# Expert blocks of 32 rows in four column tiles, with the output projection one block behind

## The reference

```python
group = argmax(h2 @ w_rg)                     # one of 4 groups for a token
top2 of softmax((h2 @ w_re)[group])           # two of its 8 experts
gates = group_gate * top_p / sum(top_p)
# every token goes to its 2 experts: 4096 slots over 32 experts
out = (silu(xb @ w_g[e]) * (xb @ w_u[e])) @ w_d[e]     # 1024 -> 512 -> 1024
x = x + sum over the two slots of gates * out
```

## Time and profile before

| | us |
|---|---|
| median of 3 runs (3032.55 to 3043.99) | 3043.69 |
| profiled execution: own time | 3044.74 |
| profiled execution: span | 3043.0 |
| TensorE busy in the span | 2849.8 (94%) |
| VectorE busy | 1205.5 (40%) |
| ScalarE busy | 997.1 (33%) |
| GpSimd busy | 657.3 (22%) |
| first expert product | 2081.0 |
| last copy of y begins | 3035.9 |

### The profile page before, as it was taken

The page is one execution under the profiler, slowest core; times in us unless marked ns, Lnnn a source line. Parts: engine busy times, 40 slices in busy tenths (PEclk is TensorE's granted clock), DMA queues, the critical chain, the costliest instruction groups (busy, mean ns, idle before and its releaser), DMA issues. The chain is left out here.

```text
span 3043.0 us, 74182 instructions
## 1 busy us (share of the span) xinstructions
PE 2849.8 (94%) x29606; PEld 1672.9 (55%) x29607; DVE 1205.5 (40%) x2075; ACT 997.1 (33%) x1998; POOL 657.3 (22%) x857
## 2 busy tenths in 40 slices
PE   8999999999999997888888889968999999999998
PEld 3444444444666664777777645544555555555554
DVE  2333311113887875677666424351111111111111
ACT  1111100002666665555545333431222222222221
POOL 0000300000110112656555200002222222222222
PEclk9999999999999998999999999978999999999999
DMA  3211131111122030111111055414868778677763
GB/s 129 69 52 58 50 114 62 62 56 72 34 67 67 8 97 16 30 47 41 40 42 43 12 189 203 156 62 154 319 224 293 244 266 285 211 237 237 265 236 76
DMA packets 172755, 374.77 MB, mean 123 GB/s; under 512 B 28386, under 2 KB 109794, under 8 KB 153475
## 3 DMA queue, kind: packets, MB, share of 16 engines
q10 hardware_dynamic: 31088, 182.46, 15.3%
q1 hardware_dynamic: 128338, 146.25, 14.8%
q0 software_dynamic: 13120, 43.00, 6.8%
HBM read 298.79 MB, written 72.88 MB: 122 GB/s over the span
## 5 line engine op out<-in xcount | busy, mean ns | idle before, releaser
L2214 PE MATMUL gu_ps<-wg_,xT 128*64 128x128 f32 (+1 forms) x1760 | 391.1, 381 | 1.8 <-issue 1.8
L2215 PE MATMUL gu_ps<-wu_,xT 128*64 128x128 f32 (+1 forms) x1760 | 391.1, 381 | 0.0
L712 DVE TENSOR_TENSOR_SCAN h_all<-h_all 128x512 f32<-128x512 f32 (+3 forms) x320 | 345.9, 1129 | 68.9 <-ACT h_all L664 42.8
L344 PE MATMUL ps<-low,high 128*128 128x512 f32 x768 | 337.3, 596 | 2.4 <-issue 2.4
L2214 PEld LDWEIGHTS gu_ps<-wg_,xT 128*64 128x64 f32 x1760 | 220.2, 137 | 191.6 <-issue 191.5
L2235 PE MATMUL y_ps<-wd_,hT 128*64 128x512 f32 x648 | 295.4, 598 | 0.0
L2234 PE MATMUL y_ps<-wd_,hT 128*64 128x512 f32 x648 | 295.4, 598 | 0.0
L2309 DVE SCALAR_TENSOR_TENSOR h<-sil,gate,gu_ps 64x384 f32<-64x384 f32 (+1 forms) x162 | 78.9, 487 | 431.3 <-ACT sil L2266 431.3
L344 PEld LDWEIGHTS ps<-low,high 128*128 128x128 f32 x768 | 144.4, 191 | 173.2 <-issue 173.2
L1707 PE MATMUL ps<-high 128*128 128x512 f32 x512 | 232.3, 604 | 7.8 <-DMA high<-mixT 7.6
L2215 PEld LDWEIGHTS gu_ps<-wu_,xT 128*64 128x64 f32 x1760 | 220.2, 137 | 0.0
(11 more groups left out here) (315 smaller groups left out, 5018.2 us busy)
## 6 DMA issues: line engine op xcount, KB each, us to landing
wd_<-in_w_exp_down ACTq DMA_DIRECT2D x29, 2048.0 KB, 18.7
wg_<-in_w_exp_gate ACTq DMA_DIRECT2D x20, 2048.0 KB, 8.8
wu_<-in_w_exp_up ACTq DMA_DIRECT2D x20, 2048.0 KB, 14.1
high<-in_w_exp_gate ACTq DMA_DIRECT2D x9, 2048.0 KB, 8.9
high<-in_w_exp_up ACTq DMA_DIRECT2D x9, 2048.0 KB, 14.1
pT<-low SPq DMA_DIRECT2D x13, 1024.0 KB, 3.9
rkv<-pT SPq DMA_DIRECT2D x96, 128.0 KB, 2.4
high<-in_x SPq DMA_DIRECT2D x16, 512.0 KB, 4.0
```

Of the source, the lines that this page charges most:

```text
L344: done = pe.matmul(qkv_ps[:, part, :], hT[:, s, k, :], w_sb[:, k, part * SBW:(part + 1) * SBW], start=(k == 0), stop=(k == KT - 1))
L712: dve.tensor_tensor_scan(prod[:, n % KEPT, h, 0:w][:, ::-1], rows, rows, so_far, ALU.mult, ALU.bypass).then_inc(scanned, 1)
L2214: pe.matmul(gu_ps[half][LO, 0:wide], xT[:, k, :], wg[s][:, k, cols], start=(k == 0), stop=(k == KT - 1))
L2215: last = pe.matmul(gu_ps[half][HI, 0:wide], xT[:, k, :], wu[s][:, k, cols], start=(k == 0), stop=(k == KT - 1))
```

## The change

- Blocks of 32 rows. Each expert has at least two blocks, and the last one's number is made so that the total is even (`n_pairs`). Tables have 196 columns for 130.
- Four column tiles of 32 columns of the array: gate's two halves of 256 columns and up's two halves side by side into the four partition quarters of one PSUM bank `gu_ps`; the output projection likewise in four quarters of 256 columns.
- The output projection of block b-1 stands behind gate and up of block b; the transposes of h of block b-1 stand in the middle of gate and up of block b.
- Rows are fetched as quarters (four partitions per row, 256 values each) and added as quarters. For that `h2` is stored with each half of a row permuted (`by_chunk`), the router's weights are read in the same order, and the tables are spread to 128 partitions by one more product. Two buffers each of `take`, `put`, `gate` and `y`; one of `xg`, `xT`, `h`, `hT`.
- An add is issued when all adds before it are done, which GpSimd itself now waits for; it no longer waits for its fetch.
- SyncE issues the weight loads, when the down product of an expert's last block is done.

The diff, cut: what is removed from `run_experts` stands in the code above.

```diff
@@ -36,10 +36,10 @@
 N_GROUPS, PER_GROUP = 4, 8
 NE = N_GROUPS * PER_GROUP
 FF = 512
-ROWS = 64
-MAX_BLOCKS = 2 * SEQ // ROWS + NE
+ROWS = 32
+MAX_BLOCKS = 2 * SEQ // ROWS + 2 * NE
 SLOTS = 3
-TABLE = MAX_BLOCKS + SEQ // ROWS + 2
+TABLE = MAX_BLOCKS + 4
 NORM_EPS, LN_X_EPS = 1e-6, 64e-5
 EXP_HALF = 0.6065306597126334
@@ -1708,6 +1708,12 @@
                              start=(k == 0), stop=(k == KT - 1))
         if half == 1 and k == KT - 1:
             done.then_inc(self.mixed, 1)
+def by_chunk(row):
+    return row.rearrange("t (p k) -> t k p", p=P)
@@ -1905,7 +1913,11 @@
                     dve.wait_ge(rooted, t + 1)
                     dve.reciprocal(rstd[:, :], root[:, :])
                     dve.drain()
-                    dve.scalar_tensor_tensor(h2[:, s, :], x_t[:, s, :], rstd[:, :], gain[:, :], ALU.mult, ALU.mult).then_inc(h2_ready, 1)
+                    for half in range(2):
+                        cols = slice(512 * half, 512 * half + 512)
+                        done = dve.scalar_tensor_tensor(h2[:, s, cols].rearrange("t (k p) -> t k p", p=P), by_chunk(x_t[:, s, cols]), rstd[:, :],
+                                                        by_chunk(gain[:, cols]), ALU.mult, ALU.mult)
+                    done.then_inc(h2_ready, 1)
                 def one_tile(t, s, n, first, last):
...
@@ place_slots @@
-                dve.tensor_scalar(blocks[:, :], blocks[:, :], 1.0, None, ALU.max)
+                dve.tensor_scalar(blocks[:, :], blocks[:, :], 2.0, None, ALU.max)
...
+                pe.wait_ge(to_ready, 1)
+                pe.matmul(to_ps[:, 0:TABLE], spread[:, :, :].rearrange("t q r -> t (q r)"), to_f[:, :], start=True, stop=True).then_inc(spread_done, 1)
...
@@ -2096,60 +2133,72 @@
     with ExitStack() as ctx:
         sb, pb, sem = makers(nc, ctx, program)
         FT = FF // P
...
+        QUARTERS = [slice(q * ROWS, (q + 1) * ROWS) for q in range(4)]
+        LO, HI = slice(0, 2 * ROWS), slice(2 * ROWS, 4 * ROWS)
         wg, wu, wd = experts.wg, experts.wu, experts.wd
         gu_loaded, d_loaded = experts.gu_loaded, experts.d_loaded
...
+        take = [sb(f"take7{j}", [P, 1], I32) for j in range(2)]
+        put = [sb(f"put7{j}", [P, 1], I32) for j in range(2)]
+        gate = [sb(f"gate7{j}", [P, 1]) for j in range(2)]
+        xg = sb("xg", [P, 2, P])
+        xT = sb("xT", [P, 2, 4, ROWS])
+        sil = sb("sil", [P, FF // 2])
+        h = sb("h7", [P, FF // 2])
+        hT = sb("hT7", [P, 2, 2, ROWS])
+        y = [sb(f"y7{j}", [P, D // 4]) for j in range(2)]
         ident = sb("ident7", [P, P])
         warm = sb("warm7", [P, 1])
...
+        xT_ps = [pb(f"xT_ps7{j}", [P, 512]) for j in range(2)]
+        gu_ps = pb("gu_ps7", [P, 512])
+        hT_ps = pb("hT_ps7", [P, 512])
         y_ps = pb("y_ps7", [P, 512])
         names = """consts gathered turned xT_ready gu_done silu_ready h_ready h_turned hT_ready
...
+        def pairs_of_blocks(eng, pairs, one_block):
+            for b in range(4):
+                one_block(b, b % 2, first=(b == 0))
+            with eng.Fori(2, pairs) as i:
+                for j in range(2):
+                    one_block(i * 2 + j, j, first=False)
+        def stores_done(eng, blocks):
+            if not isinstance(blocks, int) or blocks > 0:
+                eng.wait_ge(stored, blocks * 16)
+        give_credit(nc, y_copied)
         with nc.Block() as block:
             @block.sync
             def _(sp):
+                def refill(e, s):
+                    sp.wait_ge(y_done, start_of(sp, e + 1))
+                    experts.load(sp, e + SLOTS, s)
                 experts.load(sp, SLOTS - 1, SLOTS - 1)
...
+                with sp.Fori(0, (NE - SLOTS) // SLOTS) as i:
+                    for s in range(SLOTS):
+                        refill(i * SLOTS + s, s)
+                for e in range((NE - SLOTS) // SLOTS * SLOTS, NE - SLOTS):
+                    refill(e, e % SLOTS)
             @block.gpsimd
             def _(pool):
@@ -2158,40 +2207,42 @@
                 pool.drain()
                 pool.sem_inc(consts, 1)
...
+                def gather(j):
+                    pool.indirect_dma_start(out=xg[:, :, :].rearrange("t a b -> t (a b)"), out_offset=None, in_=h2_quarters[:, :],
+                                            in_offset=bass.IndirectOffsetOnAxis(ap=take[j][:, 0:1], axis=0)).then_inc(gathered, 16)
+                def next_rows(j, b):
+                    pool.tensor_copy(take[j][:, :], from_all[:, bass.ds(b, 1)])
+                def one_block(b, j, first):
+                    pool.wait_ge(turned, b + 3)
+                    pool.sem_inc(on_pool, 1)
+                    gather(1 - j)
+                    next_rows(j, b + 4)
+                    pool.tensor_copy(put[j][:, :], to_all[:, bass.ds(b, 1)])
                     pool.drain()
...
+                    stores_done(pool, b)
+                    pool.sem_inc(on_pool, 1)
+                    pool.wait_ge(y_copied, b * 2 + CREDIT + 2)
+                    pool.sem_inc(on_pool, 1)
+                    pool.indirect_dma_start(out=out_quarters[:, :], out_offset=bass.IndirectOffsetOnAxis(ap=put[j][:, 0:1], axis=0),
+                                            in_=y[j][:, :], in_offset=None, compute_op=ALU.add).then_inc(stored, 16)
+                pairs = pairs_of(pool)
+                next_rows(0, 0)
+                next_rows(1, 1)
                 pool.drain()
...
+                gather(0)
+                for b in (1, 2):
+                    pool.wait_ge(turned, b)
+                    gather(b % 2)
+                    next_rows(1 - b % 2, b + 1)
+                    pool.drain()
+                pairs_of_blocks(pool, pairs, one_block)
+                pool.wait_ge(gathered, pairs * 32 + 48)
+                pool.sem_inc(on_pool, 1)
+                pool.wait_ge(stored, pairs * 32)
+                pool.sem_inc(on_pool, 1)
                 pool.drain()
@@ -2199,119 +2250,129 @@
                 def turn(b):
                     pe.wait_ge(gathered, b * 16 + 16)
                     pe.sem_inc(on_pe, 1)
...
+                    for j in range(2):
+                        last = pe.transpose(xT_ps[j][:, 0:P], xg[:, j, :], ident[:, :])
                     last.then_inc(turned, 1)
...
+                def gate_up(b, s, ks):
+                    for k in ks:
+                        for q, (w, half) in enumerate(((wg, 0), (wg, 1), (wu, 0), (wu, 1))):
+                            last = pe.matmul(gu_ps[QUARTERS[q], 0:256], xT[:, k % 2, k // 2, :], w[s][:, k, half * 256:(half + 1) * 256],
+                                             start=(k == 0), stop=(k == KT - 1))
+                    if KT - 1 in ks:
+                        last.then_inc(gu_done, 1)
+                def turn_h():
+                    for j in range(2):
+                        done = pe.transpose(hT_ps[:, j * 2 * ROWS:(j + 1) * 2 * ROWS], h[HI, j * P:(j + 1) * P], ident[HI, HI])
+                    done.then_inc(h_turned, 1)
+                def down(b, s):
+                    pe.wait_ge(hT_ready, b + 1)
+                    pe.wait_ge(y_copied, b * 2 + CREDIT)
+                    for f in range(FT):
+                        for q in range(4):
+                            last = pe.matmul(y_ps[QUARTERS[q], 0:256], hT[:, f % 2, f // 2, :], wd[s][:, f, q * 256:(q + 1) * 256],
+                                             start=(f == 0), stop=(f == FT - 1))
+                    last.then_inc(y_done, 1)
+                def one_block(b, before, s, s_before):
                     pe.wait_ge(xT_ready, b * 2 + 2)
...
+                    pe.wait_ge(h_ready, b)
+                    gate_up(b, s, range(0, KT // 2))
+                    turn_h()
+                    gate_up(b, s, range(KT // 2, KT))
                     turn(b + 1)
...
+                    down(before, s_before)
+                def weights_of(s, n):
+                    pe.wait_ge(gu_loaded[s], n * 32 + 32)
+                    pe.wait_ge(d_loaded[s], n * 16 + 16)
                     pe.sem_inc(on_pe, 1)
...
+                def rest_of_expert(e, start, s):
+                    with pe.Fori(1, count_of(pe, e)) as n:
+                        one_block(start + n, start + n - 1, s, s)
+                def one_expert(e, s, n):
+                    start = start_of(pe, e)
+                    weights_of(s, n)
+                    one_block(start, start - 1, s, (s - 1) % SLOTS)
+                    rest_of_expert(e, start, s)
                 pe.wait_ge(consts, 1)
                 turn(0)
...
+                weights_of(0, 0)
+                pe.wait_ge(xT_ready, 2)
+                gate_up(0, 0, range(0, KT))
+                turn(1)
+                rest_of_expert(0, 0, 0)
+                with pe.Fori(0, (NE - 1) // SLOTS) as i:
+                    for x in range(SLOTS):
+                        one_expert(i * SLOTS + x + 1, (x + 1) % SLOTS, i + (x + 1) // SLOTS)
+                for e in range((NE - 1) // SLOTS * SLOTS + 1, NE):
```

(88 more changed lines are left out.)

220 lines of the change are left out of this document (61 added, 159 removed).

## The result

The changed kernel takes 3156.4 us (median of 4 runs, 3152.17 to 3170.48) against 3039.7 beside it: ratio 1.039, 95% interval 1.035 to 1.044. It is slower, as forecast and inside the range, but by 117 us where the sum said 39. The profiled execution took 3158.5 us, with a span of 3156.7.

The account below looks back on a forecast made before the run. TensorE's own work was taken to bound the expert stage. After the change 864 + 5 + 124 of stalls = 993 us against 955, plus 2 for routing, gives 3083 us, slower by 1.3%; range 2985 to 3165.

Parts of the forecast that it names:

- Products and turns: TensorE in the expert stage: 5.12 us of products plus 0.9 of turns, 6.0 a block, 864 us for 144 blocks, plus 5.
- rival 4: TensorE's four column tiles don't run together at the full rate: about 3690 us; chance 0.03.
- 821 to 936: Stated bounds in us for TensorE's 144 blocks, with turns of 0.6 to 1.4 us a block and 5 at the end.
- The add instruction: GpSimd's instruction for adding 128 quarter rows: bounded by 0.99 and 2.9 us, taken as 1.5.
- Rival 3: GpSimd pays by row: add instruction 2.9 us, its own round 6.2, loaded cycle 10, total 3170 us; chance 0.10.
- Routing and tables: Before the expert stage: scaling h2 in strided halves costs 2 us (0 to 4), wider tables 0 (-3 to +3).
- Fetching and adding: GpSimd's serial fetches and adds under weight loads: cycles 7.4 and 8.1 us, the slower setting the block; 124 us of stalls.
- signs named for "right": Quiet TensorE blocks of 6.0 us, about 8 after weight issues, idle before transposes or down product, GpSimd waiting for its last add.
- The rise under a load: Extra time of a fetch or add during a weight load: between 1.7 and 3.5 us, taken as 2.6 with half the bytes.
- The clock: TensorE's clock in the expert stage: at full clock before; the forecast's sum has no term for a fall.
- rival 2: Small transfers keep the whole rise under a load: cycle 9.0 us, 160 us of stalls, total 3118; chance 0.19.
- the forecast's own formula: Stalls in the expert stage: 16 us of each load over the cycle, times the cycle's excess over 6.0, times 30 loads.
- Rival 1: Small transfers slip through under loads, cycle below 6.0 us: no stalls, stage 869, 86 less, total 2960; chance 0.30.

Follow-up runs that it names:

- e8: Changed kernel without drain, weight loads in 2 KB rows, fetches two blocks ahead, two adds in flight, odd blocks' adds into an unused array: 2976 us, ratio 0.979.
- e1: Changed kernel with GpSimd's drain between the index copies and the add replaced by a semaphore that the second copy raises: 3108 us, ratio 1.023.
- e5: e1 without the adds into the output, GpSimd still waiting for each block's y: 3061 us, ratio 1.007.
- e6: e1 with only the first three fetches, later blocks reusing block 2's rows, adds kept: 3051 us, ratio 1.004.
- e11: e6 with plain writes to the same rows instead of adds: 2978 us, ratio 0.979.
- e9: e8 with all adds into the output, an expert's first block also waiting for the add just before: 2994 us, ratio 0.984.
- e4: Changed kernel without GpSimd's drain and with weight loads cut into pieces of 2 KB per row: 3066 us, ratio 1.009.
- e12: Changed kernel with GpSimd's index copies and drain ahead of the fetch instead of behind it: 3254 us, ratio 1.071.

## Why the forecast was right in sign and wrong in size

- *Products and turns*: forecast 6.0 us a block and 864 + 5; measured 6.08 in a quiet block, and 890 for the stage in which nothing is waited for (e8). 21 us short: 12 by the 0.08, the rest mostly at changes of expert, which I gave nothing. Four column tiles do run together (a group every 0.21 to 0.22 us): rival 4 is out. The bounds "821 to 936" are added up wrongly: 737 with 0.6 to 1.4 us a block and the 5 is 829 to 944.
- *The add instruction*: forecast 1.5, measured 1.60. Rival 3 is out; GpSimd is busy 419 of 1082 us.
- *Routing and tables*: forecast +2 and 0; measured +1 and -3.
- *Fetching and adding, the step that failed*. "Wait for the turn, fetch, two small copies, wait for the last add, wait for y, add": this leaves out the drain between the copies and the wait for the add. In the old order it stood behind an open wait for the fetch and cost nothing; there I had priced it, and I carried the price over. The list of changes says that an add "no longer waits for its fetch"; by its semaphores it doesn't, by the drain it does. The drain makes the add wait for the fetch, and the fetch waits behind the last add, so two cycles that I had taken side by side, 8.1 and 7.4, became one of 9.5 to 11.6 in 36 of the gaps. Taking it out gives back 55 us (e1). Of the signs named for "right", the quiet blocks and the idle time ahead of the transposes came, but GpSimd waited for its own fetch and not for its last add.
- *The rise under a load*, the second step that failed: I let it shrink to 2.6 us with the bytes, so that a loaded fetch had 6.0 us and a loaded add 7.1. It didn't shrink. Alone in the queue, 6 to 13 us into a load, the fetch rises by 3.3 us (e5), the add by 3.6 (e6), the plain write by 3.3 (e11), and the old fetch with twice the bytes rose by 3.4. In the first 5 us of a load the rises are 3.6 for the fetch, 5.0 for the add and 4.2 for the write. In the changed kernel the fetch behind its add took 8.0 there and the add 8.8. "The whole rise stays" was the better term. The Trainium skill (DMA: Bandwidth & Descriptors, "Queues, rings and completion order") has each DMA engine take the queues that have work in turn, a packet at a time. If its packets are those that the profile counts, the rise should grow with their number; from 32 to 64 it doesn't (3.3 and 3.4), and with 128 it grows by 0.3 to 1.4. The same page's fit ("Anatomy of one DMA": 2.0 us plus bytes over 436 GB/s) gives an estimate of 2.3 us for 128 KB: the plain write has 2.4, the fetch 2.8, the add 3.8, for which it has no term.
- *The clock*, a term that I put at nothing without a reason. The idle time came out near the forecast (134 us against 124 of stalls), and that is in part luck: I had some 60 blocks of 8.1 us and there are 36 of 9.5 to 11.6. The long stalls were paid again in slow products: TensorE's 14402 instructions take 884 us in e8 and 948 here, 64 us more.

Sum of what was missing, against e8: 1082.5 - 993 = 89.5 = 21.4 of products and changes of expert + 63.9 of clock + 4.2 of idle. By cause rather than place, e1 puts 55 of the 89 on the drain (38 of that being clock). What e1 leaves over, 34 us, is 21 of products and changes of expert and 26 of clock, less 13 by which its idle time falls short of the forecast. These are subtractions between traces; no run gives the unshrunk rise a price of its own. The profiled times differ by 3158.5 - 3044.7 = 114 us: 127 more in the stage, 15 less ahead of it, 2 more behind it.

By its time rival 3 (3170) lay nearest, but its mechanism is out. By mechanism rival 2 ("the whole rise stays", 3118) was nearest, and still 38 us short, since it has neither the drain nor the clock. By the forecast's own formula a cycle of 7.4 us gives 3050 and not 3040. Rival 1's mechanism shows only once the waits are taken away: e8 and e9 have the 86 us that TensorE's shorter work was to bring, less 21 and 33.

## What to carry to other kernels

Before an engine's queue gets a new order, list each thing that its drains and waits hold, transfers that it has itself issued included; a copy that must be seen by a later transfer can signal a semaphore instead. When blocks shrink, the time in flight of a small transfer hardly does (the fetch of half the bytes took 2.8 us for 3.4 quiet, and 6.1 for 6.8 under a load): give each two blocks of time, by a second buffer and by letting additions to different rows be under way together. Stalls of several microseconds on TensorE can cost half as much again in slow products behind them (64 us on 134 here), where 90 us of shorter stalls cost next to nothing (e4), so count stalls by length, not only by their sum.

## What the runs showed of the hardware

- A drain on GpSimd lasted until the indirect transfers that it had issued had landed: up to 9.1 us for fetches (the changed kernel) and up to 6.5 us for adds (e12).
- An indirect add of 128 rows of 1 KB goes as 1 KB packets, takes 1.57 us on GpSimd and 3.8 us to land; a plain indirect write of the same takes 0.98 and 2.4, in 4 KB packets (e6, e11).
- Under a weight load, 6 to 13 us into it, the old fetch (256 KB in 64 packets) and, each alone in GpSimd's queue, the new fetch, the add and the plain write (128 KB in 32, 128 and 32 packets) take 3.3 to 3.6 us longer than quiet: the rise goes neither with the bytes nor with the packets.
- A fetch issued 2.1 us after an add, early in a load, landed after 8.0 us (the changed kernel), against 6.4 without adds (e5). Distance alone doesn't explain it: 12 us into a load, 1.9 us behind an add, e1 has 6.4.
- TensorE's clock was at its upper level up to an idle stretch of 3.6 us and at the lower one in the work behind it (0.51). In a stage with 90 us of idle time in stalls of at most 2.4 us it stayed at the upper one (e4, 1.00).
